# The first eight experts' tokens gathered in two halves, and one more up matrix loaded ahead into the free half

## The reference, cut to what matters

```python
def expert_block(args):
    rows, e = args
    xb = x_pad[rows]
    h = jax.nn.silu(xb @ w_gate[e]) * (xb @ w_up[e])
    return h @ w_down[e]
...
for i in range(DEPTH):
    ...                                   # mixer, layer norm
    f = moe_ffn(x, ...)                   # router, 64 routed experts, 1 shared expert
    x = layer_norm(DN_ALPHA * x + f, ln_g[i, 1], ln_b[i, 1])
```

## Time and profile before

| | us |
|---|---|
| median of three runs | 1190.31 |
| the runs | 1190.1, 1190.31, 1192.46 |
| the profiled execution | 1190.48 |
| its span | 1188.7 |

### The profile page before, as it was taken

One profiled execution on the slowest core, in us unless ns is written; L12 is line 12 of the kernel. 1 busy time (PEld: TensorE's weight loads), 2 busy tenths in 40 slices (PEclk: granted clock), 3 DMA queues, 4 the chain that ended last, 5 costly groups with the idle time before them and its releaser, 6 DMA issues.

```text
span 1188.7 us, 30380 instructions
## 1 busy us (share of the span) xinstructions
PE 1140.5 (96%) x12940; PEld 666.2 (56%) x12942; DVE 347.1 (29%) x912; ACT 299.9 (25%) x713; POOL 56.3 (5%) x100
## 2 busy tenths in 40 slices
PE   9999999999899999998999999999999999999995
PEld 6865654555454555454777646555454555454542
DVE  0445522212122212121523556122222222221214
ACT  1454222212122212122213523122221212221212
POOL 1430100000001000000011001000000010000000
PEclk9999999999999999999999999999999999999998
DMA  9966699999999999999991556999999999999994
GB/s 377 418 261 227 213 415 425 428 428 428 427 427 423 427 424 427 426 427 407 407 424 62 243 221 222 396 426 425 429 428 427 428 420 426 425 427 426 427 422 182
DMA packets 42469, 449.51 MB, mean 378 GB/s; under 512 B 4481, under 2 KB 4865, under 8 KB 14209
## 3 DMA queue, kind: packets, MB, share of 16 engines
q1 hardware_dynamic: 41360, 443.30, 89.5%
q10 hardware_dynamic: 1008, 4.73, 1.0%
HBM read 446.96 MB, written 1.05 MB: 377 GB/s over the span
## 4 chain that ended last, share of the span: by engine, by line
PE 78%; DMA 16%; DVE 3%; issue 2%; ACT 1%; POOL 0%; DVEq 0%; SPq 0%; POOLq 0%; ACTq 0%
PE bank L1327 16%; PE bank L1355 15%; PE bank L1389 15%; DMA ring<-in_w_gate 12%; PE bank L873 7%; PE bank L892 6%; PE bank L1397 5%; PE bank L935 4%; DMA ring<-in_w_in_b 2%; DMA ring<-in_w_down 2%; PE bank L1364 1%; PE bank L1223 1%; PE bank L1094 1%; PE bank L1105 1%; PE bank L1206 1%
## 5 line engine op out<-in xcount | busy, mean ns | idle before, releaser
L1355 PE MATMUL bank<-ring,router_work 128*32 128x256 f32 x3904 | 227.6, 381 | 17.9 <-issue 17.9
L1327 PE MATMUL bank<-ring,router_work 128*32 128x256 f32 x3968 | 225.8, 379 | 8.2 <-DMA ring<-in_w_gate 8.2
L1389 PE MATMUL bank<-ring,router_work 128*32 128x512 f32 x1888 | 218.4, 595 | 0.7 <-DMA ring<-in_w_down 0.6
L1327 PEld LDWEIGHTS bank<-ring,router_work 128*32 128x32 f32 x3968 | 127.7, 110 | 119.6 <-issue 27.8
L1355 PEld LDWEIGHTS bank<-ring,router_work 128*32 128x32 f32 x3904 | 134.5, 110 | 100.3 <-issue 28.1
L2056 DVE SCALAR_TENSOR_TENSOR yhalf<-bank,gcol,yhalf 128x512 fp32r<-128x512 f32 x124 | 92.9, 751 | 214.8 <-ACT yhalf L1690 214.8
L2048 DVE TENSOR_TENSOR router_work<-router_work,bank 128x256 f32<-128x256 f32 x64 | 27.0, 422 | 359.5 <-PE bank L1355 359.5
L1690 ACT ACTIVATE yhalf<-bank,gcol 128x512 fp32r<-128x512 f32 x124 | 85.1, 688 | 168.6 <-PE bank L1389 168.6
L1389 PEld LDWEIGHTS bank<-ring,router_work 128*32 128x32 f32 x1888 | 56.1, 109 | 118.9 <-issue 110.7
L1523 ACT ACTIVATE router_work<-bank 128x256 f32<-128x256 f32 (+4 forms) x229 | 92.1, 420 | 116.3 <-PE bank L873 44.6
L1523 ACT ACTIVATE back<-bank 128x128 fp32r<-128x128 bf16 x64 | 17.8, 278 | 296.1 <-PE bank L1297 296.1
(11 more groups left out here) (184 smaller groups left out, 844.0 us busy)
## 6 DMA issues: line engine op xcount, KB each, us to landing
ring<-in_w_gate SPq DMA_DIRECT2D x58, 2048.0 KB, 19.9
ring<-in_w_down SPq DMA_DIRECT2D x56, 2048.0 KB, 20.3
ring<-in_w_up SPq DMA_DIRECT2D x52, 2048.0 KB, 21.4
ring<-in_w_up SPq DMA_DIRECT2D x18, 1024.0 KB, 12.4
ring<-in_w_in_b SPq DMA_DIRECT2D x3, 3072.0 KB, 23.5
ring<-in_w_gate SPq DMA_DIRECT2D x8, 1024.0 KB, 7.5
ring<-in_w_down SPq DMA_DIRECT2D x6, 1024.0 KB, 10.4
out_first<-in_w_out SPq DMA_DIRECT2D x2, 2048.0 KB, 28.9
```

What stands on the lines that cost most here:

```text
L1327: last = pe.matmul(gate_bank[slots_of(e, t), 0:HID], xg[:, k, slots_of(2 * j + e, t)], w[e][:, k, :], start=(k == 0), stop=(k == KT - 1))
L1355: last = pe.matmul(up_bank[slots_of(e, t), 0:HID], xg[:, k, slots_of(2 * j + e, t)], w[e][:, k, :], start=(k == 0), stop=(k == KT - 1))
L1389: last = pe.matmul(yb[half][rows_of(t, e), :], hT[b][:, f, slots_of(e, t)], w[e][:, f, half * 512:half * 512 + 512], start=(f == 0), stop= ...
```

## The change

Per layer, four things are done.

- `xg` gets a new order of columns (`gathered_slots`, `by_quad`): the first four experts of an octet (a *quad*) fill its first half for every chunk, the other four its second half.
- For the first octet of a layer `gather` is replaced by two calls of `gather_quad`: quad 0 before pair 0, quad 1 inside unit 1, between `turn_h` and `down`. A call makes 32 products of 128 columns in place of 32 of 256; the two calls make 64. `turn_h` of unit 1 moves ahead of `down`. The copies of a quad take two chunks at a time, 512 columns as before, four copies per quad.
- The second half of `xg` first takes a matrix: `up_apart` is now a pair of places, and holds both up matrices of pair 1. Pair 0's up matrices are both in the ring, and `next_up` loads both up matrices of pair 3. In sum six up matrices are loaded ahead instead of five. The transfer into `xg` follows `shared_gu` and stands ahead of the two kept matrices for `xT` and `x`; `next_up` (2 MB) is issued after `out1` is used, where 1 MB was.
- At pair 18 `reload_down` is moved ahead of the reload of pair 17's down, since its slot has long been free.

```diff
-        up_apart = work[:, 6144:8192].rearrange("p (k n) -> p k n", k=KT)
+        up_apart = [work[:, 6144:8192].rearrange("p (k n) -> p k n", k=KT), xg[:, :, HID:2 * HID]]
...
-        first_gather_bank = (0, 2, 1, 3, 0, 1, 2, 0)
+        quad_bank = ((0, 2, 1, 3), (0, 3, 1, 2))
...
             def next_up(l):
-                sp.sem_inc(sem(f"up_landed0_{l}"), 16)
-                expert(l, 1, 0, 1)
+                for k in range(UNROLL, 2 * UNROLL):
+                    sp.sem_inc(sem(f"up_landed{k}_{l}"), 16)
+                pair(l, 1, 1, 1)
...
-            def load_up_apart(l):
-                sp.dma_start(up_apart, by_k(w_up[l, 0, :, 0, :])).then_inc(sem(f"up_apart_{l}"), 16)
+            def load_up_apart(l, e):
+                sp.dma_start(up_apart[e], by_k(w_up[l, 1, :, e, :])).then_inc(sem(f"up_apart_{l}"), 16)
...
                 used(sp, (l, "out1"))
-                expert(l, 0, 3, 1)
+                next_up(l)
                 expert(l, 0, 2, 2)
                 sp.wait_ge(sem("normed"), 2 * TT * l + TT)
                 keep(l, 1, 0)
                 sp.wait_ge(sem(f"shared_gu_{l}"), TT)
+                load_up_apart(l, 1)
                 keep(l, 1, 1)
...
                 reload_gate_halves(l, 1, 1, 0)
-                sp.wait_ge(sem(f"hidden_{l}"), 1)
-                expert(l, 1, 1, 1)
+                reload_up_halves(l, 1, 1, 0)
                 reload_gate_halves(l, 2, 1, 1)
-                reload_up_halves(l, 2, 1, 1)
                 reload_down(l, 1, 1, 0)
...
                 reload(l, UNROLL * (RES_STEP - 1) + 1, RES_STEP + 1, 0)
+                reload_down(l, UNROLL * (RES_STEP - 1) + 1, RES_STEP + 1, 0)
                 reload_down(l, UNROLL * RES_STEP, RES_STEP, 1)
                 reload(l, UNROLL * RES_STEP + 2, RES_STEP + 1, 1)
-                reload_down(l, UNROLL * RES_STEP + 1, RES_STEP + 1, 0)
...
+                def gather_quad(O, q, backs):
+
+                    pe.wait_ge(s_("hot8_ready"), O + 1)
+                    for c in range(KT // 2):
...
+                        if q == 0 and c == 2:
+                            pe.wait_ge(sem("xlo"), XLO * (l + 1))
...
+                        for i in range(2):
+                            k = 2 * c + i
+                            for t in range(TT):
...
+                                first = i * 2 * QUAD_SLOTS + t * QUAD_SLOTS
+                                last = product(banks[quad_bank[q][c]][:, first:first + QUAD_SLOTS],
+                                               [(xhalf[:, part, t, k * P:(k + 1) * P], hot8[:, t, q * QUAD_SLOTS:(q + 1) * QUAD_SLOTS])
+                                                for part in range(2)])
+                        last.then_inc(s_("gathered"), 1)
...
                     for k in range(KT):
-                        if j == 0 and k == 0:
-                            chunk_out(O, 3 if first else 5)
-                        if j == 0:
+                        if place in (0, 2) and k == 0:
+                            quad_out(O, place // 2, 3 - place)
+                        if place in (0, 2) and k % 2 == 0:
+                            quad_out(O, place // 2, k // 2)
...
                     turn_back(U + 1, OCTET * o + 2 * j + 2, 1 - b)
+                    turn_h(U)
                     if place == 1:
+                        gather_quad(O, 1, U + 2)
                         down(U - 1, 1 - b, 2 * O, O + 1, U + 2, False, False)
-                    turn_h(U)
```

More of the change, by code:

```diff
@@ L596, in first_layer @@
                 pair(0, 0, 0, 2)
-                next_up(0)
-                expert(0, 0, 1, 1)
+                pair(0, 0, 0, 1)
                 load_apart(0)
@@ L604, in first_layer @@
                 pair(0, 0, 1, 0)
-                expert(0, 0, 2, 1)
                 for e in range(2):
@@ L641, in second_layer @@
                 row_pair(2)
-                used(sp, (1, "in3"))
-                next_up(1)
                 used(sp, (1, "in2"))
@@ L647, in second_layer @@
                 used(sp, (1, "in1"))
-                expert(1, 0, 1, 1)
+                pair(1, 0, 0, 1)
                 pair(1, 0, 0, 2)
@@ L651, in second_layer @@
                 pair(1, 0, 1, 0)
-                expert(1, 0, 2, 1)
                 load_shared_down(1)
@@ L720, in _ @@
                         sp.wait_ge(sem(f"rounded_{l}"), r + 1)
-                        load_up_apart(l)
+                        for e in range(2):
+                            load_up_apart(l, e)
                         with sp.Fori(1, RES_STEP) as i:
@@ L1266, in gather @@
+                def gather(O, backs):
                     pe.wait_ge(s_("hot8_ready"), O + 1)
                     for k in range(KT):
-                        earlier = [c for c in range(k) if bank_of_chunk[c] == bank_of_chunk[k]]
+                        earlier = [c for c in range(k) if gather_bank[c] == gather_bank[k]]
                         if earlier:
                             chunk_out(O, earlier[-1])
-                        if backs is None and k == 0:
-                            pe.wait_ge(sem(f"shared_silu_{l}"), TT)
@@ L1281, in gather @@
                             pe.wait_ge(s_("hT_ready"), backs)
                         for t in range(TT):
-                            if backs is None and k == 0 and t == 1:
-                                pe.wait_ge(sem("xhi"), TT * (l + 1))
-                                pe.wait_ge(sem("xlo"), XLO * l + 2)
-                            last = product(banks[bank_of_chunk[k]][:, t * 256:(t + 1) * 256],
+                            last = product(banks[gather_bank[k]][:, t * 256:(t + 1) * 256],
@@ L1309, in gate @@
                 def gate(U, O, j, rs, kept, place):
-                    b, first = j % 2, place == 0
+                    b = j % 2
                     pe.wait_ge(s_(f"gate_landed{2 * b}"), rs * 16 + 16)
@@ L1354, in up @@
                             for t in range(TT):
-                                last = pe.matmul(up_bank[slots_of(e, t), 0:HID], xg[:, k, slots_of(2 * j + e, t)], w[e][:, k, :],
+                                last = pe.matmul(up_bank[slots_of(e, t), 0:HID], xg[:, k, gathered_slots(j, e, t)], w[e][:, k, :],
                                                  start=(k == 0), stop=(k == KT - 1))
-                        if place == 1 and k == KT // 2 - 1:
+                        if place == 0 and k == KT // 2 - 1:
                             last.then_inc(s_("half_hidden"), 1)
@@ L1723, in unit @@
                         gathered(O + 1)
-                    if not first:
+                    if first and j == 1:
+                        quad_gathered(O, 1)
+                    if not first or j > 0:
                         y_out(U - 1, (j - 1) % OCT_PAIRS)
@@ L1733, in _ @@
                 with act.Fori(0, rounds) as r:
-                    gathered(r * OCTETS, first_gather_bank)
+                    quad_gathered(r * OCTETS, 0)
                     back_out(r * PAIRS, 0)
                     for j in range(OCT_PAIRS):
-                        unit(r, 0, j, first=(j == 0))
+                        unit(r, 0, j, first=True)
                     with act.Fori(1, SHARED_OCTET) as o:
@@ L2031, in _, with gathered, quad_gathered @@
                 rounds = dve.value_load(nround_i[0:1, l:l + 1], min_val=0, max_val=3) + 1
-                def gathered(O, bank_of_chunk=gather_bank):
+                def gathered(O):
                     for k in range(1, KT, 2):
                         dve.wait_ge(s_("gathered"), KT * O + k + 2)
-                        copy(by_expert(xg[:, k, :]), by_tile(banks[bank_of_chunk[k]])).then_inc(s_("xg_dve"), 1)
+                        copy(by_quad(xg[:, k, :]), by_tile(banks[gather_bank[k]])).then_inc(s_("xg_dve"), 1)
+                def quad_gathered(O, q):
+                    for c in range(1, KT // 2, 2):
+                        dve.wait_ge(s_("gathered"), KT * O + q * (KT // 2) + c + 2)
+                        copy(quad_chunks(q, c), by_two(banks[quad_bank[q][c]])).then_inc(s_("xg_dve"), 1)
                 def slot_gates(U, j):
@@ L2085, in unit @@
                     slot_gates(U + 1, (j + 1) % OCT_PAIRS)
-                    if j == 0 and not last_octet:
+                    if j == (2 if first else 0) and not last_octet:
                         one_hot8(O + 1, OCTET * o + OCTET, r)
```

64 lines of the change are left out of this document (44 added, 20 removed).

## The result

The changed kernel took 1201.76 us (median of four executions: 1198.93, 1200.46, 1203.06, 1203.61), the kernel before 1190.68 in the same comparison. The ratio is 1.0088, 95% interval 1.0074 to 1.0103: **slower by 10.5 us**, 8.8 to 12.3. The prediction said 1194.7, a loss of 4.4 us. The sign was right; of the size more than half was missing. The profiled execution took 1203.06 us with a span of 1201.3.

The account below looks back on a forecast made before the run. The DMA weight stream was taken to bound the kernel, TensorE nearly full. Delay d of 5.2 us less backlogs of 2.8 and 3.2 gave +2.4 and +2.0: +4.4 us, 1190.3 to 1194.7 us; range 1189 to 1198.3.

Parts of the forecast that it names:

- Quad 0: Half gather before gate of pair 0: same number of products and same wait for `x_low`, so no gain in time.
- d: TensorE's delay from unit 1 on, also at the transfer issued at 182.10: 0.86 + 3.8 + 0.50 = 5.2 us.
- The wait before the first gate: Gate of pair 0 writes the last chunks' bank and waits for DVE's copy: 0.86 us, same order in layer two.
- Quad 1: Unit 1: 32 more products at 0.119 us, 3.8 us with nothing beside them on TensorE.
- Rival A: Gather products: narrow ones are cheap because the load hides, 0.06 us each; 1189.0 us, not slower; chance 0.15.
- rival B: Gather products: narrow fp32r ones lose their single pass and cost 0.216 us each; 1205.1 us; chance 0.06.
- `turn_h`: Unit 1: moved ahead of `down`, the transposes lose their cover, adding 0.50 us.
- rival C: Quad 1's new place brings more waits, 1.8 us together, making d 7.0 us; 1198.3 us; chance 0.06.
- The backlog: Time TensorE could release a transfer later unnoticed by the stream: 2.8 us at 182.10, 3.2 at its layer-two twin.
- the rule: Per layer, the weight stream shifts by max(d - backlog, -2.5) us.
- the place: The transfer issued at 182.10, after the second octet's gather, taken as the narrowest place, with 2.8 us of backlog.
- The zeros: Transfer into `xg`, later `next_up`, pair 18's earlier `down` transfer and copies in twos: each taken to cost 0.

Follow-up runs that it names:

- e11: The changed kernel, unchanged, measured once more against the kernel before: ratio 1.0063, median 1198.12 us.
- after: The kernel with the whole change, against the kernel before: 1201.76 us, ratio 1.0088.
- e1: The changed kernel with three of every four products of the first half gather made 256 columns wide again, waits unchanged: 1197.25 us, ratio 1.0053 to the kernel before.
- e3: The changed kernel with 256-column products in the first half gather and its banks in order 0, 3, 2, 1: 1194.88 us, ratio 1.0033 to the kernel before.
- e5: The kernel before plus 32 narrow products per layer, results thrown away, ahead of the down products of unit 1: ratio 1.0018.
- e10: The kernel before plus 48 narrow products per layer, results thrown away, ahead of the down products of unit 1: ratio 1.0048.
- e6: The kernel before plus 64 narrow products per layer, results thrown away, ahead of the down products of unit 1: ratio 1.0093.
- e9: The kernel before with the gather split in two halves, first half's products 256 columns wide, loads as before: ratio 1.0057.
- e4: The kernel before with only the gather split in two halves, products narrow, loads as before: 1200.76 us, ratio 1.0085.
- e8: e3 with unit 3's down products ahead of the second octet's gather, and unit 1's `turn_h` between quad 1's first two chunks: ratio 1.0001 to the kernel before.
- e7: The kernel before with the second octet's gather set behind the down products of unit 3 instead of ahead of them: ratio 0.9999.
- e2: The changed kernel with the first half gather's banks in order 0, 3, 2, 1, products narrow: 1197.40 us, ratio 1.0052 to the kernel before.

## Why the prediction was wrong, step by step

- **Quad 0, "the same number of products, so no gain in time".** This is the step that failed. The count was right and so was the price at full clock (1.97 us for sixteen, e11). What the step left out is that half the columns at the same waits can take TensorE's clock down, and that it stays down over the gate that follows. Where it fell, it cost (3.08 - 1.97) + (5.37 - 3.66) = 2.8 us in layer one; in layer two, whose rows stand below, (2.60 - 1.97) + (5.87 - 3.66), again 2.8. All of it goes into d, whose cover the prediction had already spent. Between the profiled executions of after and e1 lie 6.1 us (1203.06 and 1196.93), about the 5.6 of the two layers; between the medians 4.2, since not every execution had both falls in full, and with the ratio of e11 in place of the first only 1.2. Without this loss the kernel would have lain inside the stated range (e1: 1197.25 us). No rival had this mechanism. The prediction read the clock column only as a row of ones, and asked of halved columns what they gain.
```profile
739.89 2.60 PE L870 MATMUL bank<-hot,xhalf 128*128 128x128 f32 x16 [0.52 <-DVE xhalf L1963]
743.35 5.87 PE L1355 MATMUL bank<-ring,router_work 128*32 128x256 f32 x64 [0.86 <-DVE router_work L1810]
```

- **The wait before the first gate**: predicted 0.86 us, measured 0.87. Right, and e3 against e1 (1.0033 and 1.0053) fits with its counting, though the intervals overlap.
- **Quad 1**: predicted 3.8 us at 0.119 a product, measured 3.77 at 0.118. Right. Rival A (0.06) and rival B (0.216) are refuted by the same row. The 81 ns of the Trainium skill ("TensorE: Matmul & The Clock Gate", section "Back-to-back issue gap") don't hold for this stream of fp32r products: 32 of them on new weights each take 0.118 us.
- **`turn_h`**: predicted 0.50 us, and its wait is there, 0.43. But the prediction counted only what the transposes add ahead of `down` and not what they no longer take behind it, where they stood from 153.33 to 153.76 in the kernel before. On the way to gate of pair 2 the move costs next to nothing (next point). No further wait came with the new place, so rival C, in the form it had, is refuted: the rows of unit 1 show none but this one.
- **d = 5.2 us**: 4.76 in e1, from the first gather product on (187.30 - 129.60, against 182.10 - 129.16). In the kernel after, gate of pair 1 to gate of pair 2 takes 162.13 - 146.98 = 15.15 us, and in e1 it takes 15.14, against 153.76 - 142.52 = 11.24: 3.9 longer, where the prediction said 4.3. So d was 0.4 us too large, by `turn_h`. The rows of e1:

```profile
143.86 3.66 PE L1356 MATMUL bank<-ring,router_work 128*32 128x256 f32 x64
159.00 3.64 PE L1356 MATMUL bank<-ring,router_work 128*32 128x256 f32 x64
```

- **The backlog, 2.8 and 3.2 us.** As a sum over both layers the rule agrees with the delays of 3.8 and 5.7 us (e5, e10), and with that of 7.5 in the one execution of e6 whose clock stayed up. With the split it comes out too small: for d = 5.2 it gives 4.4 us, for the 4.76 that e1 shows 3.5; measured were 6.3 (e1, 4.1 to 8.6) and 6.8 (e9, 4.8 to 8.7), so 4.4 lies just inside the one interval and just outside the other. Some 2 to 3 us of the loss are in no term of the prediction, the second share of the miss. Two of its inputs are weak: the 7.5 us for an unqueued 2 MB, made from a 1 MB transfer by the rate of a full queue, where 7.6 to 9.0 were measured (the plain correction by it is refuted by e5), and the place, since in e5 the delay was in the stream before 182.10. Of the three waits by which TensorE was to make up time, that of 1.28 us is not put down to a transfer in its row.
- **A place that the prediction didn't look at.** Part of this lies outside the loops. All eight profiles with the split (after, e1 to e4, e8, e9, e11) have a wait of 0.8 to 1.5 us for `mem_kv` between the two layers; before, e6, e7 and e10 have none there, e5 has 0.50. The row of e1:

```profile
586.63 3.72 PE L904 MATMUL bank<-ring,memT 128*128 128x256 f32 x16 [1.02 <-DMA ring<-in_w_mem_kv]
```

  The transfer is issued in its place, some 6.3 us after the wait at the end of layer one's loop, as in the kernel before, but takes longer; in e1, and then in e10, which has a like delay without the split:

```profile
ring<-in_w_mem_kv SPq DMA_DIRECT2D x1, 1024.0 KB, 16.2
```

```profile
ring<-in_w_mem_kv SPq DMA_DIRECT2D x1, 1024.0 KB, 14.9
```

  From the end of layer one's loop to the second half of the first gather in layer two, e9 thus falls back another 0.8 us behind the kernel before, and e10 catches up 0.6: 1.4 us between the two, the right size for the difference of their medians; why the split, which changes nothing near this transfer, makes it longer was not found, and no run takes it away.
- **The zeros** (transfer into `xg` in rows of 1 KB, later `next_up`, order of pair 18, copies in twos): right as a sum, by e9 against e1; they were not parted further.

Together: 4.4 predicted, 4.2 between the medians for the clock, and 1.9 more at nearly the same d make 10.5. Of the 1.9 some 0.8 lie between the layers; the cause of the rest, and of the longer `mem_kv`, stays open.

## What to carry to other kernels

Before narrowing the moving operand of products in a stretch where TensorE also waits, look at the granted clock around it: at halved columns and unchanged waits it fell here and made the next, untouched 64 instructions half again as long, while products that wrote 256 columns, half of them scratch, cost 0.1 us more for sixteen and kept the clock. Loading more ahead pays only if the engine that releases the slots keeps up; the edit of e7 is worth nothing where the stream is full, and in e8, with the transposes moved as well, 3.8 us where the engine holds it. Price an unqueued transfer by one of its own size, not by scaling a smaller one. And before an excess over a rule is explained, look at the clock of the whole execution: in e6 it had fallen far from the place that was changed.

## What the runs showed of the hardware

- The fall of the clock is not the same from one execution to the next of one kernel: both layers, layer one alone (e2, e11) or layer two alone (e4), at the same order of instructions. Which, was seen to vary; why, wasn't found. It also fell once behind an idle stretch of 1.97 us in e6 (606 us) and one of the same length in the kernel before (1147 us), over products that no version changes.
- With a new 128 x 128 operand each, 32 fp32r products of 128 moving columns took 3.77 us, or 0.118 each, and 32 of 256 columns 4.07, or 0.127 (the gather for the second octet in the kernel before). Sixteen of the narrow ones took 1.97 us, and 3.08 where the clock fell among them.
- A 2 MB transfer with nothing ahead of it landed after 7.6 us once and after 8.6 to 9.0 seven times, where 1 MB took 5.0. With a predecessor 2 to 4 us from landing, as at the fetch for the third pair in after, e1, e6 and e10, it took 8.7 to 10.0.
